# A pair of depthwise-convolution tiles made on VectorE, and the conditioning steps moved between layers

## The chip, the cores and the metric

The kernel runs on 1 core of one Trainium2 chip. The metric is the device time of one execution in microseconds; lower is better. Times shown for a kernel are the median of several runs, with the lowest and the highest.

## What is computed

The reference chains two transformer stacks on one sequence of 256 tokens of width 1024, all in float32. The first stack has a dilated-window attention layer and an mLSTM layer, each followed by a SwiGLU. The second has four layers (neighbourhood attention, conformer convolution, short gated convolution, neighbourhood attention), each followed by a squared-ReLU MLP, with a context sequence of another 256 tokens carried along; both together are the 512 columns of most of its work. Every layer of the second stack is modulated by a vector that comes from a conditioning input. What the change touches:

```
mod_l = (silu_c @ mod_w[i] + mod_b[i]).reshape(b, N_MOD, 1, D_MODEL)
...
def dwconv(x, w):
    k = w.shape[0]
    return lax.conv_general_dilated(
        x, w[:, None, :].astype(x.dtype), window_strides=(1,),
        padding=[((k - 1) // 2, k // 2)],
        dimension_numbers=("NWC", "WIO", "NWC"),
        feature_group_count=x.shape[-1])
...
def conformer_conv(h, w1, b1, dw, dwb, ln_g, ln_b, w2, b2):
    u = h @ w1 + b1
    a, g = jnp.split(u, 2, axis=-1)
    u = a * jax.nn.sigmoid(g)
    u = dwconv(u, dw) + dwb
    u = jax.nn.silu(layernorm(u, ln_g, ln_b))
    return u @ w2 + b2
...
def sq_relu_mlp(h, w1, w2):
    return jnp.square(jax.nn.relu(h @ w1)) @ w2
```

`dw` has 31 taps per channel. `mod_w` has, for each of four layers, 6 x 1024 columns of 1024.

## The kernel before

**Data.** Activations lie feature-major: 8 tiles of 128 channels (partitions) by 512 columns (256 of the sequence, 256 of the context). Float32 operands are split into a high and a low half; a product is three matmuls, high x high, high x low (lines 1411 and 1412) and weight-low x high (line 1426). Weights come in units of 1024 rows by 256 columns (1 MB): SyncE loads a unit into one of three `raw` buffers (line 1367), ScalarE writes its high half (`hi`, line 1692) and VectorE subtracts to get the low half (`lo`, line 2028), each in two pieces of 128x1024, into one of two slots. A unit of 256 columns gives two output tiles, each 8 x 3 matmuls of 512 columns. In most units the 16 matmuls with the high weights of a tile come first and the 8 with the low ones last (`late = "weights"`), so `lo` of a unit is first needed 16 matmuls into its first tile.

**The order of work.** A planner (class `Plan`) writes one list of steps. Each engine walks the list and issues its own part of every step, in order, with semaphores between engines. So the place of a step in the list is its place in every engine's queue. `take` (line 297), called at the start of a unit, puts the split of the next unit into the list and starts the load of the one after. `linear` runs a unit: matmuls of a tile, then its evacuation, then `beside`.

**Conditioning.** 4 x 48 steps `condition` make the modulation vectors: for each, VectorE multiplies a 128x1024 piece of `mod_w`, held in the single buffer MW, with the conditioning vectors and sums along the row, twice (line 2104, each with a short read of the accumulator behind it). The load of the next piece is a DMA on GpSimd's queue (line 2461, 512 KB) which waits for both. The planner spreads the steps: `beside` is called at the end of a tile and adds half of `pace` to a credit; at 1 a step is issued. `conditions_for` forces what is missing where a vector is needed. The pace is 0.65 in the SwiGLUs, 0 in the attention and mLSTM layers, and 1.38 from the MLP of layer 0 to the MLP of layer 2; these have 60, 14, 60, 28 and 60 tile ends that call `beside` (MLP 0, conformer, MLP 1, short convolution, MLP 2), and get 41, 10, 41, 19 and 41 steps. 40 steps are done when MLP 0 begins. The norm behind the conformer needs 88.

```
self.credit = min(self.credit + self.pace / 2, 2.0)
if self.credit >= 1 and not hold:
    self.credit -= 1
    self.condition()
```

**MLP 0** on 512 columns runs its units in the order up(0), up(1), down(0), up(2), down(1), up(3), down(2), down(3), four units each. An up tile is evacuated by ScalarE (ReLU, line 1977), VectorE (square, line 2432), ScalarE (high half, line 1979), VectorE (low half, line 2434); a down tile by two VectorE operations that add it to the residual X (line 2096). The last unit is run in halves by `close`: residuals (line 2075), squares on ScalarE (lines 1704 and 1724), their sum SA on GpSimd (lines 2467 and 2474), and a matmul with ones over SA (line 1475), from which the next norm comes.

**The conformer** (from line 1023). Four pairs of units c = 0..3: first the gate half (sigmoid on ScalarE, `cv_g`), then the value half (`cv_a`, line 2353), which makes U of channel tiles 2c and 2c+1. The convolution runs on TensorE: `cv_spread` copies U of a pair into UX, in four groups of 32 channels with four shifted copies each (16 DMAs on GpSimd's queue, line 2522; the last pair tile by tile and on two queues, line 1345); `cv_taps` (line 2361) expands the taps of a tile into small diagonal weights in WD, which shares its memory with NB and has two buffers; `cv_conv` (line 1614) then makes a tile in 8 x 4 matmuls of 32 columns of weights by 512 columns, and ScalarE evacuates it into CV with the bias (line 1926). The pair of tiles 2c-2 and 2c-1 is convolved behind the units of c; tiles 6 and 7 behind the loop, in halves (line 1624). `cv_total` (line 2369) adds the tiles up in SA for the layer norm; `cv_add_part` (line 2375) adds tile 6, and a matmul with ones over SA (line 1644) starts the mean.

Of the kernel before, what the change touches and what calls it, by code (L numbers as in the profile page):

```python
# [15 lines left out]
P = 128  # L16
# [77 lines left out]
def allocate(nc, ctx):  # L94
    m = Memory()
    lay, width = const_layout()

    def sb(name, shape, dt=F32, stack=ctx):
        return stack.enter_context(nc.sbuf_tensor(name, shape, dt))

    m.width = lay["amask"][0]
    m.cst = sb("cst", [P, m.width])
    m.one = sb("one", [P, P])
    m.PV = sb("PV", [P, KT, NROW])
    m.eps = sb("eps", [P, 1])
    m.C = sb("C", [P, 2, D])
    m.MW = sb("MW", [P, D])
    m.MX = sb("MX", [P, D], BF16)
    m.mod = sb("mod", [P, 4, 48, 2])
    m.gs = sb("gs", [P, 4, 2, KT, 2])  # L110
    m.gb = sb("gb", [8, 2])
    m.stat = sb("stat", [P, 64])
    m.X = sb("X", [P, KT, 512])
    m.raw = [sb(f"raw{i}", [P, 2048]) for i in range(RAW)]
    m.hi = [sb(f"hi{i}", [P, 2048], F32R) for i in range(HL)]
    m.lo = [sb(f"lo{i}", [P, 2048], F32R) for i in range(HL)]
    m.XN = sb("XN", [P, 2, KT, 512], F32R)
    m.SA = sb("SA", [P, 512])
    m.RS = sb("RS", [P, 512])
    m.NB = sb("NB", [P, 4, 512])  # L120
    m.TN, m.SQ = m.NB[:, 0:2, :], m.NB[:, 2:4, :]
    m.TB = m.NB[:, :, :].rearrange("p r (h n) -> p (r h) n", h=2)
    m.RL = m.NB
    m.WD = m.NB[:, :, :].rearrange("p (b g) (j c) -> p b (g j) c", b=2, c=32)

    def phase(*tensors):
        with ExitStack() as st:
            return [sb(n, s, d, st) for n, s, d in tensors]

    m.amask, m.rope, m.QK, m.V1, m.PB, m.PT1, m.RT, m.pos, m.ang = phase(  # L130
        ("amask", [P, 1152], F32), ("rope", [32, 2, S], F32),
        ("QK", [P, 2, 3, 2, 2, S], F32), ("V1", [P, 2, 2, 3, 256], F32), ("PB", [P, 2, 1152], F32),
        ("PT1", [P, 2, 3, 384], F32), ("RT", [32, 2, 512], F32),
        ("pos", [32, S], I32), ("ang", [32, 4, S], F32))
    m.HF, m.SG = phase(("HF", [P, 2, 22, S], F32R), ("SG", [P, 2, 2, S], F32))
    m.CB, m.QKM, m.VM, m.SO, m.HS, m.WT, m.G8, m.AC, m.HT, m.SG1, m.mmask = phase(
        ("CB", [P, KT, 260], F32), ("QKM", [P, KT, S], F32), ("VM", [P, 2, 8, P + 1], F32), ("SO", [P, KT, S], F32),
        ("HS", [P, 2, S], F32), ("WT", [P, 2, 384], F32), ("G8", [8, 8, S], F32),
        ("AC", [P, 2, 2, 8], F32), ("HT", [P, 2, 2, P], F32), ("SG1", [P, 2, S], F32),
        ("mmask", [P, 384], F32))  # L140
    m.QB, m.KB, m.VB, m.OB, m.PB2, m.PT2 = phase(
        ("QB", [P, 2, 2, 512], F32), ("KB", [P, 2, 2, 512], F32), ("VB", [P, 2, 4, 256], F32),
        ("OB", [P, 2, KT, 512], F32R), ("PB2", [P, 2, 2, 512], F32),
        ("PT2", [P, 2, 4, S], F32))
    m.H2, = phase(("H2", [P, 2, 2, KT, 512], F32R))
    m.U, m.UX, m.CV, m.AB, m.SGM, m.taps = phase(
        ("U", [P, 4, 576], F32), ("UX", [P, 2, 4, 2, 576], F32),
        ("CV", [P, KT, 512], F32), ("AB", [P, 2, 512], F32), ("SGM", [P, 2, 512], F32),
        ("taps", [P, KT, 4, 8], F32))
    m.YH, m.CG, m.UP, m.CO = phase(  # L150
        ("YH", [P, 2, KT, 512], F32R), ("CG", [P, 2, 2, 512], F32), ("UP", [P, 2, 2, 2, 258], F32),
        ("CO", [P, 2, 2, 512], F32))

    m.ps = [ctx.enter_context(nc.psum_tensor(f"ps{i}", [P, 512], F32)) for i in range(8)]
    m.sem = {n: ctx.enter_context(nc.semaphore(f"s_{n}"))
             for n in ["acc", "act", "high", "dve", "low", "pool", "ld", "x0", "x1", "cond", "mw", "mm", "taps", "ux0", "ux1", "ux6", "ux7", "uxs6", "uxs7", "pv", "ci", "pos", "cst", "tb0", "tb1", "tb2", "out"]
             + [f"raw{i}" for i in range(RAW)]}
    m.lay = lay
    return m
# [863 lines left out]
def conformer(p, layer):  # L1023
    s = p.norm(512, ("gs", layer, 0), (layer, 0))
    x = ("xn", s, 0, 512)
    p.do("tables", SIGMOID)
    p.do("cv_pads", s)

    def convolve(k):
        p.do("cv_conv", k, *p.bank())  # L1030
        p.do("cv_total", k)

    for c in range(4):
        def evac_g(t, b, u):
            p.do("cv_g", c, t, b, u)

        def evac_a(t, b, u):
            p.do("cv_a", 2 * c + t, t, b, u)
            if c == 3:
                p.do("cv_spread_one", 6 + t)  # L1040
            elif t == 1:
                p.do("cv_spread", c)
            if t == 1:
                p.do("cv_taps", 2 * c)
                if c < 3:
                    p.do("cv_taps", 2 * c + 1)

        p.linear("cv_w1_2", 0, 0, KT, 1024 + c * 256, 256, x, evac_g, outer=c == 0,
                 streams=None if c else (0, 1))
        p.linear("cv_w1_2", 0, 0, KT, c * 256, 256, x, evac_a)  # L1050
        for k in (2 * c - 2, 2 * c - 1):
            if k >= 0:
                if k == KT - 4:
                    p.do("tables", LNEXP)
                convolve(k)
                if k == KT - 3:
                    p.do("cv_taps", KT - 1)
    p.flush()
    used, rs_user, s = p.xn_used[1], p.rs_user, p.norms
    p.norms += 1  # L1060
# [151 lines left out]
def plan(known):  # L1212
# [10 lines left out]
    swiglu(p, 1)  # L1223
    p.pace = 0.0
    neighbourhood(p, 0, 0, True)
    p.pace = 1.38
    mlp(p, 0, 512)
    conformer(p, 1)
    mlp(p, 1, 512)
# [110 lines left out]
    return m.AB[:, k % 4 // 2, k % 2 * S:(k % 2 + 1) * S]  # L1340


def spread_one(e, m, k, g, signal, name):
    for i in range(4):
        e.dma_start(m.UX[32 * i:32 * i + 32, k // 2 % 2, g, k % 2, 0:572],
                    m.U[32 * g:32 * g + 32, k % 4, i:i + 572]).then_inc(*signal.says((name, k)))


def sync(e, w, m, p, T, sig):
# [659 lines left out]
def vector(e, w, m, p, dve, low):  # L2009
# [339 lines left out]
                        ALU.subtract).then_inc(*dve.says(("free", b, u), ("ob", layer, tile) if last else None))  # L2349

    def cv_a(k, t, b, u):
        w.wait_ge(("acc", b, u), ("cv_s", k), "cv_pads", ("ux", k // 2 - 2) if k >= 4 else None)
        e.scalar_tensor_tensor(
            out=m.U[:, k % 4, :].rearrange("p (s t) -> p s t", s=2)[:, :, 15:271],
            in0=m.ps[b].rearrange("p (s t) -> p s t", s=2), scalar=param(m, "cv_b1_2", k),
            in1=m.SGM[:, t, :].rearrange("p (s t) -> p s t", s=2), op0=ALU.add, op1=ALU.mult).then_inc(
            *dve.says(("free", b, u), ("cv_u", k)))

    def cv_taps(k):
        w.wait_ge("taps", "consts", ("conv", k - 2) if k >= 2 else None)  # L2360
        e.tensor_tensor(m.WD[:, k % 2, :, :],
                        m.taps[:, k, :, :].rearrange("p g j -> p (g j)").unsqueeze(2).broadcast_to([P, 32, 32]),
                        const(m, "group").unsqueeze(1).broadcast_to([P, 32, 32]), ALU.mult).then_inc(
            *dve.says(("wd", k)))

    def cv_total(k):
        if k:
            w.wait_ge(("cv_sum", k), ("cv_add", k - 1) if k > 1 else None)
            e.tensor_tensor(m.SA[:, :], m.CV[:, 0, :] if k == 1 else m.SA[:, :], m.CV[:, k, :], ALU.add).then_inc(
                *dve.says(("cv_add", k)))  # L2370

    def cv_add_part(i):
        at = slice(i * S, (i + 1) * S)
        w.wait_ge(("cv_sum", KT - 2, i), ("cv_add", KT - 3))
        e.tensor_tensor(m.SA[:, at], m.SA[:, at], m.CV[:, KT - 2, at], ALU.add).then_inc(
            *dve.says(("cv_add", KT - 2, i)))

# [59 lines left out]
    def finish(s):  # L2437
# [10 lines left out]
        "ml_weights": ml_weights, "ml_products": ml_products, "ml_cell": ml_cell, "ml_scale": ml_scale,  # L2448
        "ml_close": ml_close, "ml_conv": ml_conv, "ml_v": ml_v, "ml_outer": ml_outer, "block_out": block_out,
        "na_scores": na_scores, "na_softmax": na_softmax, "na_ctx_scores": na_ctx_scores, "na_turn": na_turn,  # L2450
        "na_mix": na_mix, "cv_a": cv_a, "cv_taps": cv_taps, "cv_total": cv_total, "cv_add_part": cv_add_part, "cv_center_part": cv_center_part,
        "cv_norm_part": cv_norm_part, "cv_silu_part": cv_silu_part, "sc_v": sc_v, "sc_conv": sc_conv, "sc_b": sc_b, "sc_halves": sc_halves, "mlp_up": mlp_up,
        "finish": finish})

# [1 line left out]
def gpsimd(e, w, m, p, T, sig):  # L2456
# [59 lines left out]

    def cv_spread(c):

        w.wait_ge(("cv_u", 2 * c + 1), ("conv", 2 * c - 3) if c >= 2 else None)
        for g in range(4):  # L2520
            for i in range(4):
                e.dma_start(m.UX[32 * i:32 * i + 32, c % 2, g, :, 0:572],
                            m.U[32 * g:32 * g + 32, 2 * (c % 2):2 * (c % 2) + 2, i:i + 572]).then_inc(
                    *sig[f"ux{c % 2}"].says(("ux", c)))

    def cv_spread_one(k):
# [63 lines left out]
def lay_out(inputs):  # L2590
# [5 lines left out]
    taps = np.zeros((32, D), np.float32)  # L2596
    taps[0:31] = np.asarray(inputs["cv_dw_2"]).reshape(31, D)
    arrays["taps"] = np.ascontiguousarray(taps.reshape(8, 4, KT, 4, 32).transpose(1, 4, 2, 3, 0).reshape(P, KT, 4, 8))
    arrays["mod_w_2"] = np.ascontiguousarray(np.asarray(inputs["mod_w_2"]).transpose(0, 2, 1))
    arrays["cond"] = np.stack([np.asarray(inputs["c_2"]).reshape(D), np.asarray(inputs["c_ctx_2"]).reshape(D)])  # L2600
    arrays["consts"] = constants()
# [15 lines left out]
```

## Time and profile before

| | |
|---|---|
| median of 3 runs | 2976.13 us (2972.68 to 2981.47) |
| profiled execution | 2974.47 us |
| its span | 2972.7 us |
| TensorE busy | 2905.0 us, 98% |
| VectorE busy | 2026.5 us, 68% |
| ScalarE busy | 1200.7 us, 40% |
| GpSimd busy | 348.1 us, 12% |
| granted TensorE clock, mean | 0.993 |

The page of the profile gives busy times by engine and the chain of work that ended last. Windows give the busy time of each engine in a stretch, in us from the span's start. A timeline lists an engine's instructions in order of time, with the idle time ahead of one in square brackets and what ended it. Names of engines: PE is TensorE, PEld its weight load, DVE is VectorE, ACT is ScalarE, POOL is GpSimd, SP is SyncE.

### The profile page before, as it was taken

Reading aid. Unit: us, or ns where it says so; the run is one execution under the profiler, and the core shown is the slowest. Engines: PE = TensorE matmul, PEld = TensorE weight load, DVE = VectorE, ACT = ScalarE, POOL = GpSimd, SP = SyncE. Lnnn points to the kernel's source line nnn. Section 1 sums busy time; section 2 is a strip of 40 time slices with the busy share of each in tenths; the row PEclk is TensorE's granted clock in tenths of the full one; section 3 lists DMA queues with packets and bytes.
Section 4 is the critical chain, followed back from the end, with each engine's and each line's share of the span. In section 5 each row is a group of like instructions: output and inputs, shape, how many; then the busy total and the mean of one; then the engine's idle time right before and its main releaser. Section 6 shows DMA issues by size and latency. Waiting matters only on the chain.

```text
span 2972.7 us, 43836 instructions
## 1 busy us (share of the span) xinstructions
PE 2905.0 (98%) x18238; PEld 2540.4 (85%) x18238; DVE 2026.5 (68%) x3284; ACT 1200.7 (40%) x1993; POOL 348.1 (12%) x542
## 2 busy tenths in 40 slices
PE   9999999999999999999999999999999999999998
PEld 9999999889997778888866888888888888877998
DVE  7776877668655567767744677777777777555665
ACT  5444544554544444222414532223243222443543
POOL 0000000000023210000231100011010000233000
PEclk9999999999999999999999999999999999999999
DMA  7444675347555414555473355554535555454453
GB/s 246 164 162 151 220 241 188 121 161 250 190 121 92 72 46 156 167 166 165 133 194 91 95 164 165 160 168 134 163 119 164 163 170 170 119 99 75 142 185 128
DMA packets 362279, 451.88 MB, mean 152 GB/s; under 512 B 12656, under 2 KB 332432, under 8 KB 362080
## 3 DMA queue, kind: packets, MB, share of 16 engines
q1 hardware_dynamic: 326976, 329.83, 34.3%
q0 software_dynamic: 34944, 118.65, 16.4%
q8 instruction: 144, 2.36, 0.3%
q10 hardware_dynamic: 160, 0.59, 0.1%
q14 instruction: 55, 0.45, 0.0%
HBM read 438.60 MB, written 1.05 MB: 148 GB/s over the span
## 4 chain that ended last, share of the span: by engine, by line
PE 84%; DVE 10%; ACT 5%; issue 1%; DMA 0%; POOL 0%; DVEq 0%; SPq 0%; ACTq 0%
PE ps L1411 23%; PE ps L1412 23%; PE ps L1426 22%; DVE lo L2028 2%; PE ps L1458 2%; PE ps L1450 2%; PE ps L1451 1%; PE ps L1614 1%; DVE NB L2059 1%; PE ps L1601 1%; PE ps L1423 1%; PE ps L1589 1%; ACT hi L1692 1%; PE ps L1407 1%; PE ps L1569 1%
## 5 line engine op out<-in xcount | busy, mean ns | idle before, releaser
L2028 DVE TENSOR_TENSOR lo<-raw,hi 128x1024 fp32r<-128x1024 f32 (+1 forms) x626 | 738.0, 1220 | 239.6 <-ACT hi L1692 238.2
L1411 PE MATMUL ps<-XN,hi 128*128 128x256 f32 (+1 forms) x2784 | 866.0, 331 | 5.7 <-DVE SO L2292 4.0
L1412 PE MATMUL ps<-XN,hi 128*128 128x256 f32 (+1 forms) x2784 | 858.1, 328 | 0.0
L1692 ACT ACTIVATE hi<-raw 128x1024 fp32r<-128x1024 f32 (+1 forms) x626 | 620.7, 1040 | 436.5 <-PE ps L1426 416.1
L1411 PEld LDWEIGHTS ps<-XN,hi 128*128 128x128 f32 x2784 | 530.9, 191 | 70.0 <-issue 14.1
L2104 DVE CUSTOM_DVE_ANT_0 MX<-MW,C 128x1024 bf16<-128x1024 f32 x384 | 477.3, 1243 | 151.0 <-DMA MW<-in_mod_w 144.0
L1412 PEld LDWEIGHTS ps<-XN,hi 128*128 128x128 f32 x2784 | 531.2, 191 | 44.5
L1426 PE MATMUL ps<-XN,lo 128*128 128x256 f32 (+1 forms) x2656 | 500.0, 331 | 0.4 <-DVE lo L2028 0.4
L1426 PEld LDWEIGHTS ps<-XN,lo 128*128 128x128 f32 x2656 | 412.8, 191 | 46.9 <-DVE lo L2028 0.6
L1411 PE MATMUL ps<-H,hi 128*128 128x512 f32 (+1 forms) x1072 | 367.1, 355 | 0.0
L1412 PE MATMUL ps<-H,hi 128*128 128x512 f32 (+1 forms) x1072 | 366.5, 354 | 0.0
L2461 POOL DMA_DIRECT2D MW<-in_mod_w x192 | 102.6, 534 | 1605.3 <-DVE mod L2104 1481.0
L1426 PE MATMUL ps<-H,lo 128*128 128x512 f32 (+1 forms) x1072 | 227.2, 354 | 0.0
L1411 PEld LDWEIGHTS ps<-H,hi 128*128 128x128 f32 x1072 | 202.7, 189 | 28.2
L1412 PEld LDWEIGHTS ps<-H,hi 128*128 128x128 f32 x1072 | 202.7, 189 | 28.2
L1426 PEld LDWEIGHTS ps<-H,lo 128*128 128x128 f32 x1072 | 180.6, 189 | 28.0
L2096 DVE SCALAR_TENSOR_TENSOR X<-ps,mod,X 128x256 f32<-128x256 f32 x244 | 107.3, 478 | 93.1 <-PE ps L1426 92.8
L1979 ACT ACTIVATE H<-NB 128x512 fp32r<-128x512 f32 (+1 forms) x128 | 74.1, 579 | 211.1 <-DVE NB L2432 211.1
L2467 POOL TENSOR_TENSOR SA<-SA,NB 128x256 f32<-128x256 f32 (+1 forms) x66 | 67.4, 1021 | 638.1 <-ACT NB L1704 636.6
L2434 DVE TENSOR_TENSOR H<-NB,H 128x512 fp32r<-128x512 f32 (+1 forms) x128 | 80.1, 626 | 82.6 <-ACT H L1979 82.6
L1450 PE MATMUL ps<-hi,XN 128*128 128x256 f32 x512 | 132.8, 295 | 2.8 <-DVE SO L2292 1.6
L1451 PE MATMUL ps<-hi,XN 128*128 128x256 f32 x512 | 127.4, 284 | 0.0
(267 smaller groups left out, 3615.7 us busy)
## 6 DMA issues: line engine op xcount, KB each, us to landing
raw<-in_mlp_w SPq DMA_DIRECT2D x128, 1024.0 KB, 5.3
MW<-in_mod_w POOLq DMA_DIRECT2D x192, 512.0 KB, 3.9
raw<-in_ffn_w_in SPq DMA_DIRECT2D x44, 1024.0 KB, 6.0
raw<-in_attn_w_in SPq DMA_DIRECT2D x36, 1024.0 KB, 4.8
raw<-in_na_wqkv SPq DMA_DIRECT2D x24, 1024.0 KB, 4.9
raw<-in_ffn_w_out SPq DMA_DIRECT2D x16, 1024.0 KB, 5.3
raw<-in_mlstm_w_in SPq DMA_DIRECT2D x12, 1024.0 KB, 5.3
raw<-in_cv_w SPq DMA_DIRECT2D x12, 1024.0 KB, 6.6
```

What stands on the lines that cost most here:

```text
L1411: e.matmul(out, whi, xhi, start=first, stop=False)
L1412: e.matmul(out, whi, xlo, start=False, stop=False)
L1426: i = e.matmul(out, wlo, xhi, start=False, stop=last)
L1450: e.matmul(out, xhi, hi[:, k, :], start=k == 0, stop=False)
L1451: e.matmul(out, xlo, hi[:, k, :], start=False, stop=False)
L1692: e.activation(hi[:, a:b], raw[:, a:b], ACT.Copy).then_inc(*high.says(("hi", j, i)))
L1979: e.activation(m.H2[:, q % 2, 0, k, 0:n], rl, ACT.Copy).then_inc(*act.says(("h2hi", layer, r)))
L2028: e.tensor_tensor(lo[:, a:b], raw[:, a:b], hi[:, a:b].bitcast(F32), ALU.subtract).then_inc(*low.says(("lo", j, i), ("spent", j) if i else ...
L2096: e.scalar_tensor_tensor(out=m.X[:, j, a:b], in0=src[:, a:b], scalar=mod_of(m, gate, j, i), in1=m.X[:, j, a:b], op0=ALU.mult, op1=ALU.add) ...
L2104: e.tensor_tensor_reduce(out=m.MX[:, :], in0=m.MW[:, :], in1=m.C[:, s, :], scale=1.0, scalar=0.0, op0=ALU.mult, op1=ALU.add, accum_out=m.m ...
L2434: e.tensor_tensor(m.H2[:, q % 2, 1, k, 0:n], rl, m.H2[:, q % 2, 0, k, 0:n].bitcast(F32), ALU.subtract).then_inc(*dve.says(("h2", layer, q, ...
L2461: e.dma_start(m.MW[:, :], T["mod_w_2"][n // 48][n % 48 * P:(n % 48 + 1) * P, :]).then_inc(*sig["mw"].says(("mod_raw", n)))
```

## The change

Tiles 0 and 1 of the convolution are made by VectorE: `cv_tap` multiplies the shifted row of U by one tap per channel and adds it to CV, 31 taps per tile, the two tiles in turn. The generator `two_on_vector` is put into the planner's background behind the units of c=0, and `advance` takes taps out of it: with adv=4, four at each tile from c=1 on, and seven behind each of the convolutions of tiles 2 to 5. `cv_spread`, `cv_taps` and `cv_conv` are no longer called for tiles 0 and 1. U has six rows (tiles 6 and 7 take those of tiles 2 and 3), so that tiles 0 and 1 stay while the taps run; AB shares memory with SGM. The totals are added in the order 2+3, 4, 5, 0, 1, 6. The pace is 0 from the conformer's norm to the end of the loop, 1.65 instead of 1.38 in MLP 0, and 1.45 from the end of the loop to the MLP of layer 2.

```diff
@@ conformer
+    p.pace = 0.0
...
     def convolve(k):
         p.do("cv_conv", k, *p.bank())
-        p.do("cv_total", k)
+        if k > 2:
+            p.do("cv_total", k, k - 1)
+
+    def two_on_vector():
+        for j in range(31):
+            for k in range(2):
+                p.do("cv_tap", k, j)
+                yield True
...
-            elif t == 1:
+            elif t == 1 and c:
                 p.do("cv_spread", c)
-            if t == 1:
+            if t == 1 and c:
                 p.do("cv_taps", 2 * c)
...
-        p.linear("cv_w1_2", 0, 0, KT, c * 256, 256, x, evac_a)
+        p.linear("cv_w1_2", 0, 0, KT, c * 256, 256, x, evac_a, adv=4)
+        if c == 0:
+            p.background.append(two_on_vector())
         for k in (2 * c - 2, 2 * c - 1):
-            if k >= 0:
+            if k >= 2:
                 if k == KT - 4:
                     p.do("tables", LNEXP)
                 convolve(k)
+                p.advance(7)
                 if k == KT - 3:
                     p.do("cv_taps", KT - 1)
+    p.drain()
+    p.pace = 1.45
+    p.do("cv_total", 0, KT - 3)
+    p.do("cv_total", 1, 0)
     p.flush()
@@ plan
-    p.pace = 1.38
+    p.pace = 1.65
     mlp(p, 0, 512)
     conformer(p, 1)
@@ vector
+    def cv_tap(k, j):
+        out = m.CV[:, k, :].rearrange("p (s t) -> p s t", s=2)
+        rows = m.U[:, k, :].rearrange("p (s t) -> p s t", s=2)[:, :, j:j + S]
+        taps = m.taps[:, k, :, :].rearrange("p g j -> p (g j)")
+        if j == 0:
+            w.wait_ge("taps", "params", "cv_pads", ("cv_u", k))
+            e.tensor_scalar(out, rows, taps[:, 0:1], param(m, "cv_dwb_2", k), ALU.mult, ALU.add).then_inc(
+                *dve.says(("cv_tap", k, j)))
+            return
+        w.wait_ge(("cv_tap", k, j - 1))
+        e.scalar_tensor_tensor(out=out, in0=rows, scalar=taps[:, j:j + 1], in1=out, op0=ALU.mult, op1=ALU.add).then_inc(
+            *dve.says(("cv_tap", k, j), ("cv_sum", k) if j == 30 else None))
```

## Rows read from the trace of the kernel before

**Rows 1.** Page: busy time by engine, and the chain's shares by engine.
```profile
PE 2905.0 (98%) x18238; PEld 2540.4 (85%) x18238; DVE 2026.5 (68%) x3284; ACT 1200.7 (40%) x1993; POOL 348.1 (12%) x542
...
PE 84%; DVE 10%; ACT 5%; issue 1%; DMA 0%; POOL 0%; DVEq 0%; SPq 0%; ACTq 0%
```

**Rows 2.** Windows of MLP 0 and unit c=1: busy by engine, clock, DMA share, GB/s.
```profile
core 0: us, PE busy (x) PEld busy (x) DVE busy (x) ACT busy (x) POOL busy (x), PEclk, DMA share, GB/s
...
1482.00:1504.00 22.00, 22.00 (x101) 17.95 (x104) 8.56 (x10) 5.29 (x6) 9.11 (x17) 1.00 0.78 200
...
1119.00:1444.00 325.00, 325.00 (x1436) 269.19 (x1435) 237.99 (x353) 99.67 (x128) 27.04 (x45) 1.00 0.52 165
```

**Rows 3.** Chain in order of time: start us, us, what; one pair's convolution.
```profile
1539.81 13.87 PE ps L1614 x128
```

**Rows 4.** Short convolution's taps (duration ns min/median/max); VectorE's timeline: start us, us, what.
```profile
L2413 DVE SCALAR_TENSOR_TENSOR CO<-UP,PV,CO x16: 750/752/754, 2053.0 to 2154.7; 128x512 f32<-128x512 f32 x16
...
1514.60 1.40 DVE L2353 SCALAR_TENSOR_TENSOR U<-ps,PV,SGM 128x512 f32<-128x512 f32 x2
...
2053.03 1.54 DVE L2413 SCALAR_TENSOR_TENSOR CO<-UP,PV,CO 128x512 f32<-128x512 f32 x2
```

**Rows 5.** VectorE's timeline behind the convolution of tile 3.
```profile
1553.75 1.23 DVE L2361 TENSOR_TENSOR NB<-taps,cst 128x1024 f32<-128x1024 f32 x1 [5.64 <-PE ps L1614]
...
1558.70 2.35 DVE L2028 TENSOR_TENSOR lo<-raw,hi 128x1024 fp32r<-128x1024 f32 x2
```

**Rows 6.** TensorE's timeline: the last third of two tiles one after the other.
```profile
1480.22 1.98 PE L1426 MATMUL ps<-XN,lo 128*128 128x512 f32 x8
...
1485.66 1.98 PE L1426 MATMUL ps<-XN,lo 128*128 128x512 f32 x8
```

**Rows 7.** Tile UX: last copies. Timelines: SA's sum (VectorE), its reader (TensorE).
```profile
L1345 POOL DMA_DIRECT2D UX<-U x16: 496/496/522, 1571.3 to 1580.2; - x16
...
1594.34 0.42 DVE L2375 TENSOR_TENSOR SA<-SA,CV 128x256 f32<-128x256 f32 x1
...
1597.23 0.70 PE L1644 MATMUL ps<-SA,one 128*128 128x256 f32 x2
```

**Rows 8.** Tile MW from 1100 to 1440 (starts, waits); VectorE's timeline, the last step.
```profile
L2104 DVE CUSTOM_DVE_ANT_0 MX<-MW,C x80: 1216/1225/2192, 1127.3 to 1433.1; 128x1024 bf16<-128x1024 f32 x80
...
  DMA MW<-in_mod_w: 27.5, 19
...
1440.13 1.21 DVE L2104 CUSTOM_DVE_ANT_0 MX<-MW,C 128x1024 bf16<-128x1024 f32 x1
```

**Rows 9.** VectorE's timeline, two steps at neighbouring down tiles; tile MW, landing times.
```profile
1217.86 1.22 DVE L2104 CUSTOM_DVE_ANT_0 MX<-MW,C 128x1024 bf16<-128x1024 f32 x1 [1.04 <-DMA MW<-in_mod_w]
...
1224.40 1.23 DVE L2104 CUSTOM_DVE_ANT_0 MX<-MW,C 128x1024 bf16<-128x1024 f32 x1 [0.97 <-DMA MW<-in_mod_w]
...
DMA to landing us min/median/max: 3.6/3.9/4.7
```

**Rows 10.** VectorE's timeline, three steps among up tiles, a tile skipped before the last.
```profile
1149.86 1.22 DVE L2104 CUSTOM_DVE_ANT_0 MX<-MW,C 128x1024 bf16<-128x1024 f32 x1
...
1156.55 1.22 DVE L2104 CUSTOM_DVE_ANT_0 MX<-MW,C 128x1024 bf16<-128x1024 f32 x1 [2.20 <-DMA MW<-in_mod_w]
...
1165.22 1.22 DVE L2104 CUSTOM_DVE_ANT_0 MX<-MW,C 128x1024 bf16<-128x1024 f32 x1
```

**Rows 11.** Timelines at the end of MLP 0, VectorE twice, then TensorE.
```profile
1441.38 2.19 DVE L2104 CUSTOM_DVE_ANT_0 MX<-MW,C 128x1024 bf16<-128x1024 f32 x1
...
1444.42 0.88 DVE L2096 SCALAR_TENSOR_TENSOR X<-ps,mod,X 128x256 f32<-128x256 f32 x2 [0.84 <-PE ps L1426]
...
1451.27 0.70 PE L1475 MATMUL ps<-SA,one 128*128 128x256 f32 x2
```

**Rows 12.** TensorE's timeline at the conformer's end, and the window behind it.
```profile
1661.20 0.70 PE L1475 MATMUL ps<-SA,one 128*128 128x256 f32 x2 [2.76 <-POOL SA L2474]
...
1662.00:1664.00 2.00, 2.00 (x10) 1.95 (x11) 0.00 (x0) 0.89 (x2) 0.00 (x0) 0.65 1.04 368
```

**Rows 13.** TensorE's timeline behind the short convolution.
```profile
2161.95 0.50 PE L1411 MATMUL ps<-YH,hi 128*128 128x512 f32 x1 [2.27 <-DVE YH L2426]
```

More of the change, by code:

```diff
@@ L145, in allocate @@
     m.H2, = phase(("H2", [P, 2, 2, KT, 512], F32R))
-    m.U, m.UX, m.CV, m.AB, m.SGM, m.taps = phase(
-        ("U", [P, 4, 576], F32), ("UX", [P, 2, 4, 2, 576], F32),
-        ("CV", [P, KT, 512], F32), ("AB", [P, 2, 512], F32), ("SGM", [P, 2, 512], F32),
+    m.U, m.UX, m.CV, m.SGM, m.taps = phase(
+        ("U", [P, 6, 576], F32), ("UX", [P, 2, 4, 2, 576], F32),
+        ("CV", [P, KT, 512], F32), ("SGM", [P, 2, 512], F32),
         ("taps", [P, KT, 4, 8], F32))
+    m.AB = m.SGM
     m.YH, m.CG, m.UP, m.CO = phase(
@@ L1046, in evac_a @@
                     p.do("cv_taps", 2 * c + 1)
-        p.linear("cv_w1_2", 0, 0, KT, 1024 + c * 256, 256, x, evac_g, outer=c == 0,
+        p.linear("cv_w1_2", 0, 0, KT, 1024 + c * 256, 256, x, evac_g, adv=4, outer=c == 0,
                  streams=None if c else (0, 1))
-        p.linear("cv_w1_2", 0, 0, KT, c * 256, 256, x, evac_a)
+        p.linear("cv_w1_2", 0, 0, KT, c * 256, 256, x, evac_a, adv=4)
+        if c == 0:
+            p.background.append(two_on_vector())
         for k in (2 * c - 2, 2 * c - 1):
-            if k >= 0:
+            if k >= 2:
                 if k == KT - 4:
@@ L1340, in squares_of, with rows_of @@
     return m.AB[:, k % 4 // 2, k % 2 * S:(k % 2 + 1) * S]
+def rows_of(k):
+    return k if k < 6 else k - 4
 def spread_one(e, m, k, g, signal, name):
@@ L1345, in spread_one @@
         e.dma_start(m.UX[32 * i:32 * i + 32, k // 2 % 2, g, k % 2, 0:572],
-                    m.U[32 * g:32 * g + 32, k % 4, i:i + 572]).then_inc(*signal.says((name, k)))
+                    m.U[32 * g:32 * g + 32, rows_of(k), i:i + 572]).then_inc(*signal.says((name, k)))
 def sync(e, w, m, p, T, sig):
@@ L2351, in cv_a @@
     def cv_a(k, t, b, u):
-        w.wait_ge(("acc", b, u), ("cv_s", k), "cv_pads", ("ux", k // 2 - 2) if k >= 4 else None)
+        w.wait_ge(("acc", b, u), ("cv_s", k), "cv_pads", ("ux", 1) if k >= 6 else None)
         e.scalar_tensor_tensor(
-            out=m.U[:, k % 4, :].rearrange("p (s t) -> p s t", s=2)[:, :, 15:271],
+            out=m.U[:, rows_of(k), :].rearrange("p (s t) -> p s t", s=2)[:, :, 15:271],
             in0=m.ps[b].rearrange("p (s t) -> p s t", s=2), scalar=param(m, "cv_b1_2", k),
@@ L2359, in cv_taps @@
     def cv_taps(k):
-        w.wait_ge("taps", "consts", ("conv", k - 2) if k >= 2 else None)
+        w.wait_ge("taps", "consts", ("conv", k - 2) if k >= 4 else None)
         e.tensor_tensor(m.WD[:, k % 2, :, :],
@@ L2364, in cv_taps, with cv_total @@
             *dve.says(("wd", k)))
[L2366 to L2370, printed above, removed]
+    def cv_tap(k, j):
[10 more added lines that the diff above has]
+            *dve.says(("cv_tap", k, j), ("cv_sum", k) if j == 30 else None))
+    def cv_total(k, other):
+        w.wait_ge(("cv_sum", k), ("cv_sum", 2) if k == 3 else ("cv_add", other))
+        e.tensor_tensor(m.SA[:, :], m.CV[:, 2, :] if k == 3 else m.SA[:, :], m.CV[:, k, :], ALU.add).then_inc(
+            *dve.says(("cv_add", k)))
     def cv_add_part(i):
         at = slice(i * S, (i + 1) * S)
-        w.wait_ge(("cv_sum", KT - 2, i), ("cv_add", KT - 3))
+        w.wait_ge(("cv_sum", KT - 2, i), ("cv_add", 1))
         e.tensor_tensor(m.SA[:, at], m.SA[:, at], m.CV[:, KT - 2, at], ALU.add).then_inc(
@@ L2450, in vector @@
         "na_scores": na_scores, "na_softmax": na_softmax, "na_ctx_scores": na_ctx_scores, "na_turn": na_turn,
-        "na_mix": na_mix, "cv_a": cv_a, "cv_taps": cv_taps, "cv_total": cv_total, "cv_add_part": cv_add_part, "cv_center_part": cv_center_part,
+        "na_mix": na_mix, "cv_a": cv_a, "cv_taps": cv_taps, "cv_tap": cv_tap, "cv_total": cv_total, "cv_add_part": cv_add_part, "cv_center_part": cv_center_part,
         "cv_norm_part": cv_norm_part, "cv_silu_part": cv_silu_part, "sc_v": sc_v, "sc_conv": sc_conv, "sc_b": sc_b, "sc_halves": sc_halves, "mlp_up": mlp_up,
@@ L2517, in cv_spread @@
     def cv_spread(c):
-        w.wait_ge(("cv_u", 2 * c + 1), ("conv", 2 * c - 3) if c >= 2 else None)
+        w.wait_ge(("cv_u", 2 * c + 1))
         for g in range(4):
@@ L2522, in cv_spread @@
                 e.dma_start(m.UX[32 * i:32 * i + 32, c % 2, g, :, 0:572],
-                            m.U[32 * g:32 * g + 32, 2 * (c % 2):2 * (c % 2) + 2, i:i + 572]).then_inc(
+                            m.U[32 * g:32 * g + 32, 2 * c:2 * c + 2, i:i + 572]).then_inc(
                     *sig[f"ux{c % 2}"].says(("ux", c)))
@@ L2598, in lay_out @@
     arrays["taps"] = np.ascontiguousarray(taps.reshape(8, 4, KT, 4, 32).transpose(1, 4, 2, 3, 0).reshape(P, KT, 4, 8))
+    arrays["taps"][:, 0:2] = taps[:, 0:256].reshape(32, 2, P).transpose(2, 1, 0).reshape(P, 2, 4, 8)
     arrays["mod_w_2"] = np.ascontiguousarray(np.asarray(inputs["mod_w_2"]).transpose(0, 2, 1))
```

## Prediction

> **What bounds the kernel now.** I read the page first: TensorE is busy for 98% of the span and 84% of the chain that ended last lies on it [rows 1]. So a microsecond of TensorE work taken out is a microsecond won, as long as nobody makes TensorE wait for it elsewhere. Then the windows by stage: in the stretches that the change touches, the MLP of layer 0 on 512 columns and the first half of the conformer, TensorE has no free time at all, while VectorE is busy for 238 of 325 us and for 8.6 of the 22 us of unit c=1 in the conformer [rows 2]. VectorE has room in both. The question is whether the order in which its work must come leaves that room usable, so the rest was read in VectorE's timeline, for what it waits for.
>
> **Part 1: the convolutions of tiles 0 and 1 leave TensorE.** A pair of tiles takes 13.87 us on TensorE, one unbroken piece of the chain [rows 3]. The pair of tiles 0 and 1 has the same 64 matmuls, so it is worth -13.9 us. Gone with it, beside other work: two evacuations on ScalarE, two weight expansions on VectorE, the 16 copies of cv_spread(0) on GpSimd's queue.
>
> **Part 2: 62 taps on VectorE.** No row shows this tap; the short convolution has the same form, 128x512 from SBUF, at 752 ns, and a pair where the second waits for the first takes 1.54 us, so 0.79 us from start to start [rows 4]. Two of this form that do not wait for each other start 0.65 us apart (1.40 less 0.75, the evacuations cv_a) [rows 4]. The taps alternate between the two tiles, so each waits for the one before the last, which has ended: I take 0.66 us, with 0.79 as the upper bound. That makes 41 us, at most 49 us, of VectorE time. A tile of 24 matmuls takes 5.44 us [rows 6]; adv=4 puts four taps on each tile from unit c=1 on, 2.6 us per tile, and 7 more behind each convolution of c=2 and c=3: 16, 16 + 14, 16 makes 62, all before the loop ends.
> Where does it pinch? Behind c=2. cv_taps(5) waits for conv(3), as today, and starts at 1553.75 [rows 5]. Behind it are now queued 15 taps and cv_total(3) in front of the split of the second unit of c=3. In the time of before: 1553.75 + 1.14 + 15 x 0.66 + 0.61 = 1565.4, against 1558.70 today [rows 5]; its halves are ready at 1566.6 and 1567.8. TensorE asks for them after two tiles and 16 of 24 matmuls from 1553.68 [rows 3, 6], at 1568.2 and, for the second half, 0.9 later. So nothing is lost, with 1.3 to 1.6 us in hand; at 0.79 us per tap 0.6 us are lost. Next in the queue cv_a(6) and cv_a(7) come 7 and 5 us later than today. The copies that they feed go out up to 1580.2 today [rows 7]; 5 us later and 3.9 us to land, taken from MW's load [rows 9], is 1589.1, and TensorE reads the first of them at 1553.68 + 4 x 5.44 + 13.87 = 1589.3 and tile 7's behind tile 6's: hidden. At 0.79 us per tap they are 9 us late and up to 2 us are lost. cv_total(0) and cv_total(1) add 1.3 us ahead of cv_add_part, whose result lies ready 2.5 us before TensorE reads it (1594.34 + 0.42 against 1597.23) [rows 7]: hidden. I book +0.2 us for the part, between 0 and +2.
> A rule of the Trainium skill speaks against the 0.66: its page VectorE: DVE Perf Modes, section The DRAIN you can't avoid, says that a next op does not start until the pipe is empty. By it 15 taps would take 11.3 us instead of 9.9 and the spare time at the split would be gone; the pair at 1.40 us speaks for overlap.
>
> **Part 3: conditioning moves into the MLP of layer 0.** This is the expensive part. `beside` adds half the pace at each of 60 tile ends: 60 x 0.69 = 41 steps today (40 started up to 1433 and one at 1440.13 [rows 8]) and 60 x 0.825 = 49 after. A step costs VectorE 2.4 us, which there is room for. But MW is one buffer: its next load goes out when VectorE has done both halves of the step, and takes 3.9 us to land (3.6 to 4.7) [rows 9]. VectorE, which is in order, stands before the next step until then: steps at neighbouring tiles start 6.54 us apart in one place and 6.69 in another, both with the idle time ahead of them put down to MW [rows 9, 10], and not 5.44. Today a skipped tile follows after one to three steps and pays that back. At a pace of 1.65 only one tile in 5.7 is skipped.
> Count the gaps. From the first step to the last (tile 0 to the last but one, 49 steps, 48 gaps), 38 gaps lie between neighbouring tiles and 10 skip a tile. A neighbouring gap is at least c, the MW cycle. A skipping gap in the down projections is too. In the up projections VectorE's own work fills it: one split, two gated evacuations, one step, 8.67 us without a pause for PE (1156.55 to 1165.22) [rows 10]; 5 of the 10 are such. With c = 6.65, nearer the longer row because landings stray further up than down: 43 x 6.65 + 5 x 8.67 = 329.3 us. Today these ends lie 312.9 us apart (1127.3 to 1440.13) [rows 8]. So the last step starts 16.4 us later, whatever TensorE does. TensorE feels it in two ways, in the same sum: the split halves come late from about the tenth unit on (today a split is ready, behind a residual and a step, 0.9 + 2.4 + 2.3 = 5.6 us after a tile's end, and asked for two tiles and 16 matmuls after it, at 14.5: 9 us of slack), and what is left falls due at the stage's end, where the residual of the last tile, the split and the squares stand behind the last step, and TensorE's sums at 1451.27 behind them [rows 11]. The residual waits 0.84 us for TensorE today [rows 11]; that goes: 16.4 - 0.8 = 15.6 us. Steps that meet a GpSimd add take 2.19 us for a half instead of 1.22 [rows 11]; three more steps of the chain lie in that last stretch: +2 (0 to 3). Idle gaps of this size can cost clock: behind one of 2.76 us the granted clock was 0.65 in a 2 us window [rows 12], the lower of the levels 1.2 and 2.4 GHz for part of it: +1 (0 to 3). Together +18.6 us.
> Bounds: c = 6.54 and nothing for the extras, 10.9 us; c = 6.80 with all extras, 28 us.
>
> **Part 4: what follows.** In the conformer one step is left of ten; no one waits for them on TensorE today, so nothing is won there. Pace 1.45 makes 43, 20 and 39 steps in MLP 1, the short convolution and MLP 2, against 41, 19 and 41. The same count of gaps stays below TensorE's time there, since every third or fourth tile is skipped: 0. At the end of the short convolution a step stands today ahead of sc_halves and TensorE waits 2.27 us [rows 13]; by the new count that step falls away at that tile but one stands a tile earlier: -1 (0 to -2.3).
>
> **Sum** against the profiled execution's 2974.5 us: -13.9 + 0.2 + 18.6 - 1.0 = +3.9, so 2978.4 us. The median of the three runs lies 1.7 us above that execution, inside their spread of 8.8 us, and I don't add it.
>
> **Rivals.** (a) The full gain: the extra steps stay hidden, 2974.5 - 13.9 - 1 = 2959.6. It holds if 43c + 43.3 is at most 312.9, c at most 6.27 us. Every neighbouring gap of before that I looked at is above that; for it speaks only that TensorE never waited in this stage so far. The Trainium skill, DMA: Bandwidth & Descriptors, section Anatomy of one DMA, gives 2.0 us plus bytes/436e3: 3.2 us for MW's 512 KB, an estimate by which c would be 5.95 and this rival would win; the trace has 3.9 and decides.
> (b) Some of it is made up: the stalls overlap waits that I count twice, or the lag is worked off in the close's free time; loss of 5 to 12 us, about 2970.
> (c) Slower: the denser MW loads meet more weight traffic (DMA share is 0.52 already [rows 2]) and land later. Each 0.1 us of c is 4.3 us; from c = 6.77 on the kernel is slower by over 0.3%, and at 6.80 with the extras and late copies in the conformer it ends at 2974.5 - 13.9 + 28 + 2 = 2990.6.
> (d) The change doesn't do what it says: the taps hold VectorE so long that the convolutions of tiles 6 and 7 wait. Bounded in part 2 by 2 us; it is in the sum.
>
> **How the numbers follow.** Forecast (loss of 12 to 24 us in the MLP) 0.57, own range 2972 to 2984; (a) 0.18; (b) 0.12; (c) 0.13. A measurement of this kernel can tell about 0.3%, 8.9 us, from no change. Faster by more: (a) and a little of (b), 0.20. Slower by more, above 2983.4: 0.14. Within: 0.66. The range takes in (a) and most of (c): 2959 to 2987.
>
> **What would show it.** Part 1: 13.9 us fewer on L1614's successor, no TensorE idle time from c=1 to the end of c=3. Part 2: taps 0.66 us apart; the split behind conv(3) some 7 us later. Part 3: 49 steps in the MLP, neighbouring ones 6.6 to 6.7 us apart for long stretches, VectorE idle time on MW far above today's 27.5 us [rows 8] in this stage, TensorE waiting on `lo` in the second half of the stage and for 3 to 6 us on SA at its end. I am wrong if the MLP keeps its length: then c or the slack is misjudged.

## The result and the profile after

The changed kernel takes 2984.6 us (median, 2980.6 to 2990.5) against 2976.6 us (2972.7 to 2981.6) for the kernel before, measured side by side: a ratio of 1.0023, 95% interval 1.0015 to 1.0032. That is 7 us slower by the ratio, less than the 0.3% set as the bound. The profiled execution has a span of 2982.4 us against 2972.7. The convolution gave what it was meant to give; the MLP ahead of the conformer took it back, and half as much again.

The page, as in [rows 1]: busy times by engine, then the chain's shares by engine and by line (lines after the change lie some 21 further down up to the conformer's taps, 33 behind them).

```profile
PE 2899.0 (97%) x18110; PEld 2537.7 (85%) x18110; DVE 2062.3 (69%) x3344; ACT 1196.6 (40%) x1991; POOL 340.3 (11%) x526
...
PE 74%; DVE 14%; ACT 5%; DMA 4%; issue 2%; POOL 0%; DVEq 0%; SPq 0%; ACTq 0%; POOLq 0%
PE ps L1432 20%; PE ps L1433 20%; PE ps L1447 19%; DMA MW<-in_mod_w 4%; DVE lo L2049 4%; DVE MX L2125 3%; PE ps L1479 2%; PE ps L1471 2%; PE ps L1472 1%; DVE NB L2080 1%; PE ps L1622 1%; ACT hi L1713 1%; PE ps L1444 1%; PE ps L1610 1%; PE ps L1635 1%
```

TensorE works 6 us less and its share of the chain falls from 84% to 74%. What came in is 4% of DMA, all of it the load of MW, and 3% for the conditioning itself on VectorE: a loop through load and step has become the bound somewhere. The window of MLP 0, the answer to the last line of [rows 2], shows where:

```profile
1119.00:1444.00 325.00, 317.45 (x1376) 257.62 (x1375) 239.01 (x363) 91.04 (x121) 24.39 (x46) 0.99 0.53 167
```

TensorE, with no idle time there before, has 7.6 us of it, in a stage that now ends later still. VectorE is no busier in these 325 us than before (239.0 against 238.0): it had 20 us more to do and couldn't. The tile MW over the whole stage, as in [rows 8] and [rows 9], says what held it: 49 steps, and 64.1 us of VectorE's idle time instead of 27.5. The load itself is no slower (median 3.8 us against 3.9).

```profile
L2125 DVE CUSTOM_DVE_ANT_0 MX<-MW,C x98: 1216/1225/2191, 1127.5 to 1463.5; 128x1024 bf16<-128x1024 f32 x98
...
  DMA MW<-in_mod_w: 64.1, 33
...
DMA to landing us min/median/max: 3.4/3.8/5.1
```

Two lines of VectorE's timeline at the stage's end, the last two steps: ahead of both VectorE is idle on MW, and the first half of the first one takes 2.05 us instead of 1.22, beside an addition on GpSimd.

```profile
1453.61 2.05 DVE L2125 CUSTOM_DVE_ANT_0 MX<-MW,C 128x1024 bf16<-128x1024 f32 x1 [0.30 <-DMA MW<-in_mod_w]
...
1462.24 1.23 DVE L2125 CUSTOM_DVE_ANT_0 MX<-MW,C 128x1024 bf16<-128x1024 f32 x1 [0.75 <-DMA MW<-in_mod_w]
```

The last step starts at 1462.24, 22.1 us later than in [rows 8]. And TensorE's timeline, its longest idle times from 1200 us to the stage's end (two of 1.49 and 1.44 us at 1257.15 and 1383.41 and one of 0.69 us are left out):

```profile
1222.49 2.33 PE L1447 MATMUL ps<-H,lo 128*128 128x512 f32 x8 [1.65 <-DVE lo L2049]
...
1292.76 3.21 PE L1447 MATMUL ps<-H,lo 128*128 128x512 f32 x8 [2.04 <-DVE lo L2049]
...
1472.43 1.22 PE L1496 MATMUL ps<-SA,one 128*128 128x256 f32 x2 [6.85 <-POOL SA L2507]
```

The low halves of the weights come late in five places, the first in the tenth unit, and at the end the sum of squares, which stands behind the last step on VectorE, is 6.85 us late. It starts at 1472.43 where [rows 11] had 1451.27: 21.2 us.

In the conformer, by contrast, TensorE waits for nothing between 1476 and 1608 us. The timeline of VectorE behind the convolution of tile 3, which answers to [rows 5]:

```profile
1563.07 1.23 DVE L2382 TENSOR_TENSOR NB<-taps,cst 128x1024 f32<-128x1024 f32 x1 [5.64 <-PE ps L1635]
1564.21 5.38 DVE L2397 SCALAR_TENSOR_TENSOR CV<-U,taps,CV 128x512 f32<-128x512 f32 x8
...
1570.11 4.73 DVE L2397 SCALAR_TENSOR_TENSOR CV<-U,taps,CV 128x512 f32<-128x512 f32 x7
1574.74 2.37 DVE L2049 TENSOR_TENSOR lo<-raw,hi 128x1024 fp32r<-128x1024 f32 x2
```

Eight taps take 5.38 us and 15 of them lie ahead of the split, which starts 11.7 us behind the weight expansion, 6.7 us later than before.

### The profile page after: what moved, and what is told of

It is laid out like the page before. It is cut to its first block, busy times and chain, and to the rows that moved or that the text cites. A ratio compares the mean times of both kernels' runs of the same rounds, so it can differ in the third digit from the quotient of the medians.

```text
span 2982.4 us, 43621 instructions
## 1 busy us (share of the span) xinstructions
PE 2899.0 (97%) x18110; PEld 2537.7 (85%) x18110; DVE 2062.3 (69%) x3344; ACT 1196.6 (40%) x1991; POOL 340.3 (11%) x526
## 4 chain that ended last, share of the span: by engine, by line
PE 74%; DVE 14%; ACT 5%; DMA 4%; issue 2%; POOL 0%; DVEq 0%; SPq 0%; ACTq 0%; POOLq 0%
PE ps L1432 20%; PE ps L1433 20%; PE ps L1447 19%; DMA MW<-in_mod_w 4%; DVE lo L2049 4%; DVE MX L2125 3%; PE ps L1479 2%; PE ps L1471 2%; PE ps L1472 1%; DVE NB L2080 1%; PE ps L1622 1%; ACT hi L1713 1%; PE ps L1444 1%; PE ps L1610 1%; PE ps L1635 1%
```

## The experiments

One reading per run carries most of the comparison: the time from the first step of MLP 0 to TensorE's sums at the stage's end (324.0 us before, 344.9 after), and from these sums to the first centring operation of the conformer's layer norm (147.5 us before, 135.7 after).

**The taps alone.** Pace 1.38 throughout, ten steps left in the conformer.

```diff
-    p.pace = 0.0
...
-    p.pace = 1.45
...
-    p.pace = 1.65
+    p.pace = 1.38
```

> The taps alone: tiles 0 and 1 on VectorE as in the changed kernel, but conditioning at the old pace of 1.38 everywhere, so 41 steps in MLP 0, ten in the conformer. Theory (the taps give 13.9 us, the extra steps in MLP 0 took it back): MLP 0 keeps the length of before, TensorE's sums at its end start at 1451.3 us as before, and the ratio is below 1. In the conformer ten steps of 2.4 us and their waits on MW now stand between the taps, with 1.3 us in hand at the split behind the third tile's convolution, so I expect 5 to 9 us of TensorE waits there and some 2969 us, ratio 0.997. Rival 1 (steps in the conformer cost nothing, the move was not needed): 2963 us, 0.995. Rival 2 (the taps themselves are what made the change slow): no faster than before, and the waits lie in the conformer.

Measured: 2972.9 us, ratio 0.9990 (0.9977 to 1.0002): 3.9 us of median above the figure given, and not faster clear of noise. The profiled execution was the slowest of the ten (2983.2 us) and is 8.8 us behind the kernel before already at the first step of MLP 0, so it is read by stages. MLP 0 takes 324.0 us, as before. In the conformer VectorE's timeline has the first of these lines and TensorE's the second:

```profile
1537.26 1.22 DVE L2123 CUSTOM_DVE_ANT_0 MX<-MW,C 128x1024 bf16<-128x1024 f32 x1 [10.17 <-DMA MW<-in_mod_w]
...
1570.67 3.78 PE L1445 MATMUL ps<-XN,lo 128*128 128x512 f32 x8 [6.17 <-DVE lo L2047]
```

The 6.17 us are the split behind the 15 taps, as the place was named; its 8 matmuls then took 3.78 us instead of 1.98. With three more waits of 1.24 to 1.29 us, all at convolutions, TensorE waits for some 10 us, just above the 5 to 9 us expected. A step of 2.4 us stands ahead of those taps, but it is not all that made the split late. VectorE was behind already: it had stood idle for 10.17 us on a load of MW that was issued right behind the 16 copies of `cv_spread` and took 10.9 us to land. The kernel before has the same, a load of 10.1 us and 10.55 us of idle time at 1534.96, and there TensorE doesn't wait for it. So rival 1 falls: with the taps there, steps at their old places in the conformer do cost TensorE time. Rival 2 is not refuted by this run alone, since both its signs are there, no clear gain and waits in the conformer; but from the sums to the centring it is 146.6 us against 147.5 before, so the taps are no loss, and the next two runs put the loss elsewhere.

**The move alone.** The kernel before with the three paces of the change.

```diff
+    p.pace = 0.0
...
+    p.pace = 1.45
...
-    p.pace = 1.38
+    p.pace = 1.65
```

> The move of the conditioning alone: convolution of tiles 0 and 1 on TensorE as before, paces 1.65 in MLP 0, 0 in the conformer, 1.45 behind it. Theory (one MW buffer, neighbouring steps 6.65 us apart): TensorE's sums at the end of MLP 0 start at 1472.4 instead of 1451.3, and the time is 21 us + 1.7 us of low clock - 1.3 us behind the short convolution above before: 2998 us, ratio 1.007. Rival (the extra steps hurt only together with the taps): 2976 us, 1.000.

Measured: 3000.7 us, ratio 1.0083 (1.0068 to 1.0099). MLP 0 takes 345.9 us from first step to sums, and the wait at its end is there without a single tap in the kernel:

```profile
1471.24 1.22 PE L1477 MATMUL ps<-SA,one 128*128 128x256 f32 x2 [6.80 <-POOL SA L2476]
```

From the sums to the centring it is 149.5 us, 2.0 more than before: the clock (below). By the ratio the move alone costs 24.7 us (20 to 30), and the changed kernel lost some 21 beside its gain of 14. So the loss belongs to the move.

**A second buffer for the pieces of mod_w in MLP 0.** Steps stay where they are; odd pieces go to their own buffer and semaphore, each load is issued two steps ahead.

```diff
-    m.H2, = phase(("H2", [P, 2, 2, KT, 512], F32R))
+    m.H2, _, m.MW2 = phase(("H2", [P, 2, 2, KT, 512], F32R), ("gap", [P, D], F32), ("MW2", [P, D], F32))
...
-        w.wait_ge(("mod_part", n - 1, 1) if n else None)
+        w.wait_ge(("mod_part", n - 2 if PAIRED[0] + 1 < n <= PAIRED[1] else n - 1, 1) if n else None)
```

> The changed kernel with a second buffer for the pieces of mod_w in MLP 0, so that the next piece is loading while a step runs; same 49 steps at the same tiles, nothing else changed. Theory (it is the wait for the single buffer): VectorE's idle time on MW in MLP 0 falls from 64 us to under 5, steps at neighbouring tiles start 5.4 to 5.6 us apart, the sums at the end of MLP 0 start at 1451 to 1453, TensorE's waits on lo there are gone: 2984.6 - 21 - 1.7 = 2962 us, ratio to before 0.995. Rival (VectorE simply has too much work in MLP 0, 49 x 2.4 us more or less): TensorE waits stay, over 2975 us.

Measured: 2962.5 us, ratio 0.9954 (0.9941 to 0.9967): faster than both kernels. VectorE's waits on MW in the stage and TensorE's sums at its end:

```profile
  DMA MW<-in_mod_w: 2.1, 1
...
1452.89 0.70 PE L1507 MATMUL ps<-SA,one 128*128 128x256 f32 x2 [0.19 <-POOL SA L2518]
```

The same 49 steps on the same VectorE, on average 5.5 us apart where tiles are neighbours, 2.1 us of waits on MW, and the stage takes 324.3 us. This settles between a wait and too much work: it was the wait.

**43 steps in MLP 0, five placed by hand in the conformer.**

```diff
             p.do("cv_g", c, t, b, u)
+            if (c, t) == (1, 1):
+                p.condition()
...
+            if c == 0 or (c, t) == (2, 1):
+                p.condition()
...
+                if k == KT - 4:
+                    p.condition()
...
-    p.pace = 1.65
+    p.pace = 1.45
```

> The changed kernel with pace 1.45 instead of 1.65 in MLP 0 (43 steps) and five further steps put by hand where VectorE stood idle in the conformer: two at c=0, one at the end of the gate unit of c=1, one ahead of cv_taps(4), one behind the convolution of tile 4. Theory: 43 steps stay below the saturation of MW, MLP 0 ends as before (1451 to 1452), and the conformer shows no more TensorE waits than the changed kernel: 2976.6 - 13.9 - 1 = 2962 us, ratio 0.995. Rival (any five more steps in MLP 0 or the conformer cost what was won): over 2970 us.

Measured: 2967.3 us, ratio 0.9973 (0.9958 to 0.9988). MLP 0 takes 324.0 us, as expected; the conformer does not stay clear. A sixth step came from credit left over, so three stand at c=0, waiting 4.55 and 3.37 us on MW. VectorE reaches cv_a(3) at 1511.97, 6.6 us after its tile is ready, the copies start late, and the convolution of tile 2 waits:

```profile
1532.68 16.32 PE L1641 MATMUL ps<-UX,NB 128*32 128x512 f32 x128 [5.59 <-DMA UX<-U]
```

The pair took 16.32 us instead of 13.87 behind that wait. The next run, with two steps at c=0 and none in the units behind it, has no such wait.

**46 steps in MLP 0** (pace 1.55), two at c=0: the one placed here and one from credit left over.

```diff
+            if (c, t) == (0, 1):
+                p.condition()
...
-    p.pace = 1.65
+    p.pace = 1.55
```

> The changed kernel with pace 1.55 in MLP 0 (46 steps, one tile in 4.3 skipped) and one more step at c=0 of the conformer, ahead of the first tap. Theory (MW saturates only when the skipped tiles no longer pay back 1.2 us per neighbouring pair): the same recurrence that gives +17 us for 49 steps gives no TensorE wait at all for 46, so from the first step of MLP 0 to TensorE's sums at its end it is 324 us as before (345 in the changed kernel), and the time is 2962 to 2964 us, ratio to before 0.995. Rival (the loss grows with the number of steps, 8 more cost 21 us, so 5 more cost about 13): 2976 us.

Measured: 2966.6 us, ratio 0.9964 (0.9952 to 0.9976), 3 us above the expected figure in the median; MLP 0 takes 325.0 us with one wait:

```profile
1453.00 0.70 PE L1498 MATMUL ps<-SA,one 128*128 128x256 f32 x2 [0.98 <-POOL SA L2509]
```

Five steps more than before cost 1.0 us, eight cost 20.9. The loss is a threshold, as the count of gaps had it (the "recurrence" of the expectation), and not a slope.

**48 steps in MLP 0** (pace 1.60), none in the conformer.

```diff
-    p.pace = 1.65
+    p.pace = 1.6
```

> The changed kernel with pace 1.60 in MLP 0 (48 steps; 88 done at the conformer, none in it). Theory: TensorE waits for lo 0 to 1.5 us in all, but the last four tiles before the end of MLP 0 all have a step, so the last step starts 9 to 11 us later than before and the wait for SA at the stage's end is 8 to 11 us; first step to sums 334 to 336 us; time 2973 to 2976 us, ratio 0.999. If the number of steps alone decided, it would be 2.6 us faster than the changed kernel: 2982 us; if a single step less took MW out of saturation, 2963 us.

Measured: 2982.2 us, ratio 1.0016 (1.0006 to 1.0025). MLP 0 takes 337.8 us, 2 above the range given; the waits for `lo` are 3.4 us in all, more than the 0 to 1.5 expected, and the one at the end is 7.56 us, a little less than the 8 to 11. The total is 6 us above the range given, and the profile shows where, at the end of the short convolution:

```profile
1465.89 1.22 PE L1496 MATMUL ps<-SA,one 128*128 128x256 f32 x2 [7.56 <-POOL SA L2507]
...
2169.80 0.79 PE L1432 MATMUL ps<-YH,hi 128*128 128x512 f32 x1 [6.71 <-DVE YH L2459]
```

The wait of [rows 13], 2.27 us before and 1.0 in the changed kernel, is 6.71 here. The credit carried on from MLP 0 moves later steps to other tiles: the last two ahead of sc_halves stand at neighbouring tiles here (2159.92 and 2166.64), 6.7 us apart, and VectorE is 3.6 us idle on MW before the second; in the changed kernel they are 9.2 us apart (2156.53 and 2165.77). So the expectation was wrong in leaving the stages behind as they were. That the median is just the 2982 us given for "the number of steps alone decides" is chance: MLP 0 is 7.1 us shorter than in the changed kernel and not 2.6, and the short convolution takes 5.7 us of it back.

| kernel | steps in MLP 0 | VectorE idle on MW there | first step to sums |
|---|---|---|---|
| before | 41 | 27.5 | 324.0 |
| placed by hand | 43 | 37.4 | 324.0 |
| pace 1.55 | 46 | 51.8 | 325.0 |
| pace 1.60 | 48 | 60.9 | 337.8 |
| changed kernel | 49 | 64.1 | 344.9 |
| changed, second buffer | 49 | 2.1 | 324.3 |

## Why the prediction was right, point by point

The forecast was +3.9 us, slower but inside 0.3%; it is +8.0 in the medians and +7 by the ratio. The mechanism and its place are shown by three runs that agree: the move alone brings the loss, a second buffer takes it away, fewer steps take it away. The span of the profiled executions grew by 9.7 us: 0.2 up to the first step, 20.9 in MLP 0, -11.8 from the sums to the centring (-14.1 and 2.3 of clock) and 0.4 behind it. Against the forecast part 3 is 4.6 us larger and part 4 1.4 us, both to the same side, so no large error hid another. The size was met less well than the sign: 2984.6 us is just outside the 2972 to 2984 that the forecast had as its own, and the range of 2959 to 2987 took in the full gain as well.

**Part 1**, -13.9 us: in the runs without late steps, the second buffer and pace 1.55, sums to centring take 133.4 us against 147.5, that is -14.1. TensorE has 128 instructions fewer, 18110 against 18238: the trace shows the pair's 64 matmuls as the 128 of [rows 3].

**Part 2**, taps at 0.66 us: eight in 5.38 us and one of them 0.75 gives 4.63 / 7 = 0.66 us from start to start. The split was forecast 6.7 us later and is 6.7 us later. No wait followed, as booked. How much was in hand can be read from the taps-alone run: there the split starts some 8 us later behind the convolution than here, and TensorE waits 6.17 of them, so about 1.8 us were in hand where 1.3 to 1.6 were booked. The taps start before the one ahead has ended. The sentence of the Trainium skill's page VectorE: DVE Perf Modes, section The DRAIN you can't avoid, that was weighed there is not all that the section says: it adds that a next op that is not held back starts earlier. The trace agrees with that: if each tap had waited for the end of the one ahead, the 15 would have taken 11.3 us, and they took 10.1.

**Part 3** is where the size was off: +18.6 us booked, and 20.9 us up to the sums plus 2.0 to 2.3 of clock measured, 23.

- The chain from first to last step was put at 329.3 us, with 2 for collisions 331.3; it is 334.7 us. The 38 gaps between neighbouring tiles sum to 255.2 us, 6.7 each, close to the 252.7 forecast even with the longest in them. These are 8.63 us from 1453.61 to 1462.24, where both halves of the step meet an addition on GpSimd, the 2 us booked for collisions; and 7.91 and 7.06 us, behind two loads that took 5.1 and 4.2 us to land. The ten skipping gaps were mis-sized: 76.6 forecast, 79.6 measured. One of 7.91 us, between an up and a down projection, was booked at 6.65. And among up tiles the row of [rows 10] that I took, 8.67 us, was one without a wait ahead of the split for ScalarE's high half of the weights (0.36 us behind the first of these lines); four of the five such gaps in the changed kernel are 9.12 us or more, the fifth 8.68:

```profile
1154.16 1.22 DVE L2125 CUSTOM_DVE_ANT_0 MX<-MW,C 128x1024 bf16<-128x1024 f32 x1
...
1163.28 1.22 DVE L2125 CUSTOM_DVE_ANT_0 MX<-MW,C 128x1024 bf16<-128x1024 f32 x1
```

- The end of the stage: 11.14 us from last step to sums before, 10.19 now, so 0.95 won where 0.84 was booked.
- Clock: +1 booked with 3 as the bound. Behind the wait of 6.85 us the granted clock was 0.50, which is 1.2 GHz, in this window and in the next of 2 us, and 0.56 in the third; sums to centring is 2.3 us longer than in the second-buffer kernel with the same taps.

```profile
1472.00:1474.00 2.00, 1.57 (x5) 1.31 (x5) 0.00 (x0) 0.00 (x0) 0.37 (x1) 0.50 0.87 255
```

**Part 4**, -1 us: the wait behind the short convolution fell from 2.27 to 1.0 us, but from the centring to the end it is 1374.3 us against 1373.9. Whatever was won is lost again in small waits, none of them over 1 us apart from those of before.

**The rivals.** (a) needed an MW cycle of 6.27 us or less; only the closest gap among neighbours in the changed kernel is that short, and the mean is 6.7. The estimate of 3.2 us for such a load from the Trainium skill's page DMA: Bandwidth & Descriptors, section Anatomy of one DMA, is met by no load here: the least is 3.4 us, the median 3.8. What (a) would bring, 2959.6 us, is within 3 us of what the second buffer gave. (b) had no part in it. (c) named slower loads as its mechanism, and in the median they were not slower (3.8 us against 3.9, two of 48 late): the size went its way for other reasons, the skipping gaps and the clock. (d) was rightly small.

## What to carry to other kernels

When background work with a prefetch of its own is spread over a busy engine, compare the cycle of the prefetch (issue, landing, use, release) with the spacing of the slots, not the engine's busy share: VectorE had a quarter of its time free and still couldn't take eight more steps of 2.4 us. Below saturation such steps were free here and above it each cost about a whole cycle of 6.65 us (12.8 us for the two from 46 to 48, 7.1 for the 49th), so either give the prefetch a second buffer or keep count of how many neighbouring slots are taken, above all in the last few ahead of a stage's end. And a pace that carries its credit on moves later steps to other tiles, so that stages which weren't touched have to be read again.

## What the runs showed of the hardware

A wait of 2.04 us was enough for TensorE's granted clock to fall: the 8 matmuls at 1292.76 took 3.21 us instead of 1.98, this window around them shows 0.68, and its second half, 1294 to 1296, shows 0.50, which is 1.2 GHz. In the run of the move alone the same place shows 0.50 behind a wait of 2.33 us.

```profile
1292.00:1296.00 4.00, 3.24 (x9) 2.41 (x10) 3.30 (x5) 1.12 (x2) 0.00 (x0) 0.68 0.72 189
```

Behind the wait of 1.65 us at 1222.49 the granted clock stayed at 1.00. The 2.33 us of the 8 matmuls there are not clock: the first and the fifth took 0.50 us, the others 0.39 to 0.40. In [rows 13] a wait of 2.27 us was followed by a granted clock of 1.00 too. What decides between this one and the one of 2.04 us stays open: no run was made for it.

A load of MW, 3.8 to 3.9 us in the median, took 10.1 us in the kernel before and 10.9 us with the taps alone where it was issued right behind the 16 copies of `cv_spread`.
